# A first group with both keys in one tile, head weights in fp32 column groups, and first loads without waits

## The reference, cut to what matters

```
xn = rmsnorm(h, norm_g)
aq, ak, av, agate, iq, ik, iw, cq, ckv, kr, bgate, mg = split_proj(xn @ w_in)
ik = rope(ik, IDX_ROT)      # 64 columns, key of the indexer
iw = iw * IDX_HEADS ** -0.5 # 16 columns, one weight per head of the indexer
kr = rope(kr, ROPE_DIM)     # 64 columns, rotary key of the second branch
score = sum over heads of relu(iq . ik * IDX_DIM ** -0.5) * iw
```

## Time and profile before

| | |
|---|---|
| median of 3 runs | 825.13 us (824.22 to 826.7) |
| profiled execution | 825.64 us, of which the span shown by the profile is 823.8 |
| mean granted TensorE clock | 0.998 of full speed |
| TensorE busy | 810.5 us, 98% of the span |
| VectorE, ScalarE, GpSimd busy | 524.4, 360.1, 47.2 us |
| moved by DMA | 139.84 MB, 170 GB/s over the span |

### The profile page before, as it was taken

The page is one execution under the profiler, slowest core; times in us unless marked ns, Lnnn a source line. Parts: engine busy times, 40 slices in busy tenths (PEclk is TensorE's granted clock), DMA queues, the critical chain, the costliest instruction groups (busy, mean ns, idle before and its releaser), DMA issues.

```text
span 823.8 us, 14766 instructions
## 1 busy us (share of the span) xinstructions
PE 810.5 (98%) x5953; PEld 769.8 (93%) x5953; DVE 524.4 (64%) x845; ACT 360.1 (44%) x527; POOL 47.2 (6%) x53
## 2 busy tenths in 40 slices
PE   7999999999999999999999999999999999999996
PEld 7999999999999998999999999999999999876774
DVE  5798866899876565456544444556566666645665
ACT  6734444453455583244433434343443333334433
POOL 1222102013100000000000000000000000100001
PEclk9999999999999999999999999999999999999999
DMA  9956345544633466134574555455545545464323
GB/s 319 348 179 204 118 154 175 173 132 153 205 106 113 150 255 196 53 103 138 174 251 153 165 182 163 154 159 165 185 138 169 160 151 199 157 265 160 147 103 115
DMA packets 114356, 139.84 MB, mean 170 GB/s; under 512 B 2785, under 2 KB 99041, under 8 KB 113633
## 3 DMA queue, kind: packets, MB, share of 16 engines
q1 hardware_dynamic: 112384, 131.61, 48.8%
q0 software_dynamic: 1776, 7.53, 2.5%
q10 hardware_dynamic: 144, 0.01, 0.0%
HBM read 135.44 MB, written 3.69 MB: 169 GB/s over the span
## 4 chain that ended last, share of the span: by engine, by line
PE 96%; DMA 1%; DVE 1%; ACT 1%; issue 0%; SPq 0%; ACTq 0%; DVEq 0%
PE ps L551 25%; PE ps L550 25%; PE ps L552 25%; PE ps L896 4%; PE ps L898 3%; PE ps L897 3%; PE ps L908 2%; PE ps L747 1%; PE ps L653 1%; PE ps L719 1%; PE ps L702 1%; DMA raw<-in_w_small 1%; PE ps L708 1%; PE ps L738 1%; PE ps L706 1%; DMA x_t<-in_x_t 0%
## 5 line engine op out<-in xcount | busy, mean ns | idle before, releaser
L947 ACT CAST w_hi<-raw 128x1024 fp32r<-128x1024 f32 (+1 forms) x232 | 239.9, 1041 | 324.6 <-PE ps L552 255.5
L1272 DVE TENSOR_TENSOR w_lo<-raw,w_hi 128x1024 fp32r<-128x1024 f32 (+1 forms) x232 | 280.7, 1229 | 155.0 <-ACT w_hi L947 153.3
L550 PE MATMUL ps<-x_hi,w_hi 128*128 128x288 f32 x1248 | 371.3, 298 | 4.2 <-DVE x_lo L1299 4.2
L551 PE MATMUL ps<-x_lo,w_hi 128*128 128x288 f32 x1248 | 368.1, 295 | 0.0
L552 PE MATMUL ps<-x_hi,w_lo 128*128 128x288 f32 x1248 | 367.8, 295 | 0.0
L550 PEld LDWEIGHTS ps<-x_hi,w_hi 128*128 128x128 f32 x1248 | 234.7, 188 | 6.7 <-DVE w_lo L1295 4.5
L551 PEld LDWEIGHTS ps<-x_lo,w_hi 128*128 128x128 f32 x1248 | 234.7, 188 | 0.2
L552 PEld LDWEIGHTS ps<-x_hi,w_lo 128*128 128x128 f32 x1248 | 234.5, 188 | 0.0
L552 PE MATMUL ps<-og_hi,w_lo 128*128 128x288 f32 x256 | 75.9, 296 | 0.0
L550 PE MATMUL ps<-og_hi,w_hi 128*128 128x288 f32 x256 | 75.7, 296 | 0.0
L551 PE MATMUL ps<-og_lo,w_hi 128*128 128x288 f32 x256 | 74.6, 292 | 0.0
(11 more groups left out here) (256 smaller groups left out, 758.0 us busy)
## 6 DMA issues: line engine op xcount, KB each, us to landing
raw<-in_w_in SPq DMA_DIRECT2D x76, 1024.0 KB, 5.0
raw<-in_w_out SPq DMA_DIRECT2D x16, 1024.0 KB, 5.0
raw<-in_w_o_a SPq DMA_DIRECT2D x8, 1024.0 KB, 5.0
raw<-in_w_o_b SPq DMA_DIRECT2D x8, 1024.0 KB, 5.2
raw<-in_w_uv SPq DMA_DIRECT2D x4, 1024.0 KB, 5.6
raw<-in_w_uq SPq DMA_DIRECT2D x4, 768.0 KB, 4.7
raw<-in_w_ukt SPq DMA_DIRECT2D x2, 1024.0 KB, 6.2
raw<-in_w_uk SPq DMA_DIRECT2D x2, 1024.0 KB, 5.0
```

Source lines behind the costliest of these rows:

```text
L550: nc.tensor.matmul(out, hi, x_h, start=first, stop=False)
L551: nc.tensor.matmul(out, hi, x_l, start=False, stop=False)
L947: nc.scalar.copy(w_hi[:, step % 2, cols], raw[:, step % RAW, cols]).then_inc(hi_done, pieces_done(q))
L1272: nc.vector.tensor_tensor(w_lo[:, step % 2, cols], raw[:, step % RAW, cols], w_hi[:, step % 2, cols].bitcast(F32), ALU.subtract)\
```

## The change

The unused columns go: `w_small` becomes 128 columns, ik in the first 64 and kr in the last 64, so the first group has one tile (three matmuls per k), in PSUM bank 4. The head weights get a 16-column input of their own, `w_iw`, loaded by ScalarE's queue. GpSimd clears a tile with 32 columns per k (`w_iwg`) and writes `w_iw` times `norm_g` into 16 of them. TensorE multiplies it with the uncast `x_t` in plain fp32, k modulo 4 choosing a group of 32 output partitions of bank 5, in three visits: k = 0 to 3 before the first group's k = 4, k = 4 to 7 before k = 8, and k = 8 to 15 before k = 12. VectorE scales all 128 rows of bank 5 into `iw_q`, and three matmuls with `sel`, which has four identity matrices of 16 columns below each other, add the four partial sums and turn them, in place of the transposes. SyncE issues all twelve first loads without a wait, and the first load of G_IQ in two halves of four k, each with a semaphore.

```
+def small_cols(k, n):
+    first = 1024 * (k % KH // QUARTER) + P * (k % QUARTER)
+    return slice(first, first + P * n)
...
-        small = ps[:, 4:6, 0:NTOK]
+        small = ps[:, 4, 0:NTOK]
...
             for i, (k0, n) in enumerate(PARTS):
-                if i >= 3:
-                    sp.wait_ge(x_landed[i - 3], 16)
-                dst = raw[:, k0 // KH, 256 * (k0 % KH):256 * (k0 % KH + n)].rearrange("p (k n) -> p k n", k=n)
+                dst = raw[:, k0 // KH, small_cols(k0, n)].rearrange("p (k n) -> p k n", k=n)
...
                 if j < 2:
                     sp.wait_ge(x_landed[len(PARTS) - 3 + j], 16)
+                if j == 0:
+                    for p, done in enumerate((first_landed, raw_landed[2])):
+                        dst = raw[:, 2, 1024 * p:1024 * p + 1024].rearrange("p (k n) -> p k n", k=PIECE)
+                        sp.dma_start(dst, w_in[:, PIECE * p:PIECE * p + PIECE, col:col + 256]).then_inc(done, 16)
+                    continue
...
             pool.memset(ones[:], 1.0).then_inc(ones_set, 1)
+            pool.memset(w_iwg[:], 0.0).then_inc(iw_cleared, 1)
+            pool.wait_ge(iw_cleared, 1)
+            pool.wait_ge(consts_landed, 16)
+            pool.wait_ge(iw_landed, 16)
+            pool.tensor_tensor(w_iwg[:, :, 0:IDX_HEADS], w_iw[:],
+                               norm_g[:].rearrange("p (k o) -> p k o", o=1).broadcast_to([P, KD, IDX_HEADS]), ALU.mult)\
+                .then_inc(iw_weighted, 1)
...
+            pool.dma_start(sel[:], d["sel"]).then_inc(ident_landed, 16)
...
+            pool.wait_ge(iw_ready, 3)
...
+            def head_weights(parts):
+                pe.wait_ge(iw_weighted, 1)
+                for i in parts:
+                    pe.wait_ge(x_landed[i], 16)
+                    k0, n = PARTS[i]
+                    for k in range(k0, k0 + n):
+                        c = 32 * (k % 4)
+                        last = nc.tensor.matmul(ps[c:c + 32, 5, 0:NTOK], w_iwg[:, k, :], x_t[:, k, :], start=k < 4,
+                                                stop=k >= KD - 4)
+                last.then_inc(iw_ready, 1)
             for k in range(KD):
-                half, row_tile = k // KH, k % KH
+                if k and k % QUARTER == 0:
+                    head_weights({4: (0, 1), 8: (2, 3), 12: (4, 5)}[k])
...
-                for m in range(2):
-                    cols = slice(m * P, (m + 1) * P)
-                    last = three(small[:, m, :], hi[:, row_tile, cols], lo[:, row_tile, cols], x_hi[:, k, :],
-                                 x_lo[:, k, :], k == 0, k == KD - 1)
+                hi, lo = (w[:, half, small_cols(k, 1)] for w in (w_hi, w_lo))
+                last = three(small, hi, lo, x_hi[:, k, :], x_lo[:, k, :], k == 0, k == KD - 1)
...
-                last = nc.tensor.transpose(ps[0:n, 6, tt * P:(tt + 1) * P], ik_z[:, t0:t0 + n], ident[:])
+                last = nc.tensor.matmul(ps[0:n, 6, tt * IDX_HEADS:(tt + 1) * IDX_HEADS], iw_q[:, t0:t0 + n], sel[:],
+                                        start=True, stop=True)
...
+                if isinstance(it, int) and q == 4:
+                    act.wait_ge(first_landed, 16)
+                else:
+                    act.wait_ge(raw_landed[step % RAW], landed(step, it))
...
+                if group == G_SMALL:
+                    nc.scalar.copy(z_stage[:, 0, 0, :], small)
+                    nc.scalar.copy(z_stage[0:ROPE, 0, 1, :], small[ROPE:2 * ROPE, :]).then_inc(pair_read, 1)
+                    return
...
             act.dma_start(norm_g[:], d["norm_g"]).then_inc(consts_landed, 16)
+            act.dma_start(w_iw[:], d["w_iw"]).then_inc(iw_landed, 16)
...
-            settled(nc.vector.tensor_tensor(ik_z[64:P, :], z[64:P, :], x_rstd[64:P, 0, :], ALU.mult))
+            dve.wait_ge(iw_ready, 3)
+            settled(nc.vector.tensor_tensor(iw_q[:], ps[:, 5, 0:NTOK], x_rstd[:, 0, :], ALU.mult))
```

More of the change, by code:

```diff
@@ L265, in hybrid_layer @@
         x_t, _ = at("x_t", [P, KD, NTOK], at_y)
-        x_sq, x_ss, x_var, x_root, d_end = row(at_x, ("x_sq", [P, KD, NTOK]), ("x_ss", [P, NTOK]), ("x_var", [P, NTOK]),
-                                               ("x_root", [P, NTOK]))
+        x_sq, x_ss, x_var, x_root, w_iw, w_iwg, d_end = row(at_x, ("x_sq", [P, KD, NTOK]), ("x_ss", [P, NTOK]), ("x_var", [P, NTOK]),
+                                               ("x_root", [P, NTOK]), ("w_iw", [P, KD, IDX_HEADS]),
+                                               ("w_iwg", [P, KD, 32]))
         assert d_end <= at_y
@@ L273, in hybrid_layer @@
             ("work", [P, 3, PAST + DEC]))
-        cq_hi, cq_lo, ckv_tok, iw_tok, top8, iw_four, _ = row(
+        cq_hi, cq_lo, ckv_tok, iw_tok, top8, iw_four, sel, _ = row(
             at_l, ("cq_hi", [P, KL, NTOK], F32R), ("cq_lo", [P, KL, NTOK], F32R), ("ckv_tok", [P, 3, LORA]),
-            ("iw_tok", [P, 3, IDX_HEADS]), ("top8", [P, 2, 8]), ("iw_four", [P, 4]))
+            ("iw_tok", [P, 3, IDX_HEADS]), ("top8", [P, 2, 8]), ("iw_four", [P, 4]),
+            ("sel", [P, IDX_HEADS]))
         ckv_past, score, s_end = row(at_y, ("ckv_past", [P, KL, PAST]), ("score", [P, 3, PAST + DEC]))
@@ L280, in hybrid_layer @@
         lora_z, _ = at("lora_z", [P, 2, KL, NTOK], at_f)
-        ik_t, ik_z, kr_swap, _ = row(at_x, ("ik_t", [P, NKEY]), ("ik_z", [P, NTOK]), ("kr_swap", [P, NTOK]))
+        ik_t, ik_z, kr_swap, iw_q, _ = row(at_x, ("ik_t", [P, NKEY]), ("ik_z", [P, NTOK]), ("kr_swap", [P, NTOK]),
+                                           ("iw_q", [P, NTOK]))
         ckv_hi, ckv_lo, _ = row(at_x, ("ckv_hi", [P, KL, NKEY], F32R), ("ckv_lo", [P, KL, NKEY], F32R))
@@ L366, in hybrid_layer @@
         quarters_moved = sem("quarters_moved")
+        iw_landed, iw_cleared, iw_weighted, iw_ready, first_landed = (
+            sem(n) for n in ("iw_landed", "iw_cleared", "iw_weighted", "iw_ready", "first_landed"))
         ident_landed, idx_out = sem("ident_landed"), sem("idx_out")
@@ L614, in _ @@
                 pe.wait_ge(xlo_done, k + 1)
-                hi, lo = weights(half, KH)
-                for m in range(2):
-                    cols = slice(m * P, (m + 1) * P)
-                    last = three(small[:, m, :], hi[:, row_tile, cols], lo[:, row_tile, cols], x_hi[:, k, :],
-                                 x_lo[:, k, :], k == 0, k == KD - 1)
+                hi, lo = (w[:, half, small_cols(k, 1)] for w in (w_hi, w_lo))
+                last = three(small, hi, lo, x_hi[:, k, :], x_lo[:, k, :], k == 0, k == KD - 1)
                 if k % QUARTER == QUARTER - 1:
@@ L944, in piece_hi @@
                 step, cols = q // 2, piece_cols(q)
-                act.wait_ge(raw_landed[step % RAW], landed(step, it))
+                if isinstance(it, int) and q == 4:
+                    act.wait_ge(first_landed, 16)
+                else:
+                    act.wait_ge(raw_landed[step % RAW], landed(step, it))
                 act.wait_ge(step_done, freed_by(q) + 2 * RAW * it)
@@ L961, in to_stage @@
                     act.wait_ge(stage_used, group - 3)
-                src = small if group == G_SMALL else pair(group)
-                nc.scalar.copy(z_slot(group), src).then_inc(pair_read, 1)
+                nc.scalar.copy(z_slot(group), pair(group)).then_inc(pair_read, 1)
             act.dma_start(norm_g[:], d["norm_g"]).then_inc(consts_landed, 16)
+            act.dma_start(w_iw[:], d["w_iw"]).then_inc(iw_landed, 16)
             act.wait_ge(ones_set, 1)
@@ L1289, in _ @@
             for i, (k0, n) in enumerate(PARTS):
-                half, cols = k0 // KH, slice(256 * (k0 % KH), 256 * (k0 % KH + n))
+                half, cols = k0 // KH, small_cols(k0, n)
                 if i in (0, 2):
@@ L1830 @@
     w = arrays["in_w_in"]
-    first = np.concatenate([w[:, COL_IK:COL_IK + P], w[:, COL_KR:COL_KR + P]], axis=1)
-    arrays["in_w_small"] = np.ascontiguousarray(first.reshape(KD, P, 2 * P).transpose(1, 0, 2))
+    first = np.concatenate([w[:, COL_IK:COL_IK + IDX_DIM], w[:, COL_KR:COL_KR + ROPE]], axis=1)
+    arrays["in_w_small"] = np.ascontiguousarray(first.reshape(KD, P, P).transpose(1, 0, 2))
+    head_weights = w[:, COL_IW:COL_IW + IDX_HEADS]
+    arrays["in_w_iw"] = np.ascontiguousarray(head_weights.reshape(KD, P, IDX_HEADS).transpose(1, 0, 2))
+    arrays["in_sel"] = np.ascontiguousarray(np.tile(np.eye(32, IDX_HEADS, dtype=np.float32), (4, 1)))
     past_k = arrays["in_cache_a_k"].reshape(PAST, A_KV, A_DIM)
```

7 lines of the change are left out of this document (4 added, 3 removed).

## The result

The changed kernel takes 822.74 us (median of 16 runs, 822.34 to 824.62), the kernel before, run beside it, 826.07 (16 runs, 823.81 to 827.24). The ratio is 0.9969, 95% interval 0.9962 to 0.9977: about 2.6 us of 825 are gone (1.9 to 3.1). The ratio is not the quotient of the two medians, which would be 0.9960: the 16 runs of the kernel before fall into two bunches, seven of 823.8 to 825.2 and nine of 826.0 to 827.2. By the medians 3.3 us are gone, against the 825.13 from which the prediction subtracts it is 2.4, and the profiled executions, 825.64 (span 823.8) and 822.36 (span 820.6), are 3.3 apart. Forecast were 4.45. So the direction was right and the size was not, by whichever of these measures.

A forecast was written before the change was run, and what follows sets the result against it. TensorE was taken to bound the kernel (96% of the chain), with data landings setting G_IQ's start after the change. Savings 4.8 - 0.2 - 0.15 = 4.45 us from the median 825.13 gave 820.7 us, range 819.3 to 823.0.

The forecast's parts named there:

- 4.8 - 0.2 - 0.15 = 4.45: Whole saving in us: earlier G_IQ start, less a stall at its second step, less extra records of the sel matmuls.
- Saving 22.27 - 17.5 = 4.8: First stage: G_IQ's first matmul moves from 22.27 to 17.5 us, saving 4.8, from 4.0 to 5.6.
- rival (b): Head weights: the column groups run in turn, TensorE needs 14.8 us, kernel at 823.5; chance 0.04.
- Rival (c): First loads: without waits they disturb one another, x_t's last part lands at 15 to 17, kernel 822.3 to 824.3; chance 0.08.
- Rival (d): First stage into G_IQ: TensorE's clock falls to 1.2 GHz; beyond 13.9 us of it, over 0.3% slower; chance 0.06.
- 825.13 - 4.45: Whole kernel: the saving of 4.45 us subtracted from the median of the kernel before gives 820.7 us.
- The landing of the fifth token part, 11.2: First loads: token part five (k = 8 to 11) lands at 11.2 us, between 10.5 and 11.9.
- Until 8.0 us 8.0 x 258 GB/s = 2.06 MB: First loads: bytes moved by 8.0 us in the earlier profile, from which the new landing times were worked out.
- SyncE's waits: beyond the rate above this saves nothing: First loads: dropping SyncE's three waits gains nothing beyond the assumed 0.375 MB/us, as the queue was nearly full before.
- What could be late next: G_IQ's second step: second half of the first w_in load lands near 17.0, TensorE stalls 0.2 us, at most 1.2.
- rival (a): G_IQ's second step: second half-load or the squares chain is late, 1 to 2 us given back, 821.7 to 822.7; chance 0.13.
- `sel`, I take 0.15 (0 to 0.5): Turning the head weights: three fp32 matmuls need two records each instead of one, 0.15 us more.

The follow-up runs named there:

- e9: The kernel before the change, unchanged, run once more for a second profile; 824.96 us (one run, span 823.2).
- e3: Changed kernel with head weights of k = 0 to 3 only, twelve of the sixteen fp32 matmuls left out; 822.57 us, ratio 0.9959.
- e1: Changed kernel with the old loads: SyncE's waits before the last six first loads back, first w_in load in one transfer; 824.98 us, ratio 0.9998.
- e2: Kernel before with the new loads alone: no waits before the first loads, first w_in load in two halves; 824.17 us, ratio 0.9982.
- e4: Changed kernel with three transposes and a VectorE sum over the four column groups in place of the matmuls with sel; 822.62 us, ratio 0.9961.
- e5: Changed kernel with token part five (k = 8 to 11) loaded in two transfers, a semaphore each; 822.83 us, ratio 0.9973.
- e8: Changed kernel with the w_iw transfer issued after ScalarE's first table load instead of ahead of it; 822.79 us, ratio 0.9976.
- e18: Changed kernel, unchanged, once more on another chip; 822.90 us (6 runs), ratio 0.9968.
- e15: Changed kernel with later rope table, 16 warm-up matmuls, token part five split, transposes plus VectorE sum for sel, without three VectorE rotary products; time not in the text.

## Why the prediction was wrong: the path held, the sizes on it did not

**The step that failed** is the sum "4.8 - 0.2 - 0.15 = 4.45", above all its first term, "Saving 22.27 - 17.5 = 4.8". G_IQ began at 18.10 and not at 17.5, which leaves 4.17 us in the pair of profiles, and only 3.45 against e9, in which G_IQ of the kernel before began near 21.55. `sel`, put at 0.15, measured 0.48, and a wait in VectorE's block near 60 us, which the sum lacked, took 0.18. The wait and the path that were forecast are the ones found; these errors all went the same way.

**What held.** TensorE's work of the first group fell to 48 matmuls and 32 records in three visits; the column groups run four at once (0.62 for four matmuls, 1.11 for eight; with the 0.10 ahead of each visit, which the forecast of 0.8, 0.8 and 1.3 had counted in, 0.72 and 1.21); in turn four alone would have been 1.9 us, so rival (b) is out. That the start of G_IQ is set by data and not by TensorE holds: e3 takes two visits away and moves it by 0.03. ScalarE's and VectorE's chain from the token part's landing to G_IQ was forecast at 6.3 us (17.5 less 11.2) and measured 6.31. The x_t part's last transfer landed at 13.85 (5.94 + 7.9; forecast 13.4, 12.7 to 14.1). Rival (c), that the unwaited loads disturb one another, did not come in its strong form: without the new loads the gain is gone (e1). In a weak form it may have: fewer bytes had moved by 8 us in e2 too (term 2). Rival (d), the clock, did occur, in three profiles of variants (e4, e5, e8), for 3 to 4 us only; as TensorE had time to spare there, it cost 0.2 us of G_IQ's start at most, and the case beyond 13.9 us never came.

**The terms one by one**, in the order of the sum:

1. "825.13 - 4.45", with 4.45 read from a profile of 825.64. The 22.27 of that profile holds 0.7 us of late landings that e9 does not have. Against the ratio this is the largest single error; against the difference of the medians, 3.3 us, it is none, so how much of it is an error rests on one more profile of a kernel whose runs spread over 3 us. The prediction saw the 0.5 between profile and median and passed over it; a saving that ends in a landing time can't be taken from one execution and subtracted from the median of others.
2. The landing of the fifth token part, 11.2, was 11.79: G_IQ at 18.10, 0.6 us. It was within its own bounds (10.5 to 11.9), but the middle was wrong, and it was so before 8 us already: the fourth part, put at 8.2, landed near 8.9, where SyncE's next issue, which waits for it, stands. The table by stretch of after:

```profile
0.00:8.00 8.00, 5.13 (x27) 4.76 (x28) 2.57 (x6) 4.43 (x10) 1.50 (x7) 1.00 0.73 223
8.00:14.00 6.00, 4.92 (x41) 3.58 (x41) 4.90 (x12) 4.81 (x11) 0.00 (x0) 1.00 1.04 395
14.00:30.00 16.00, 15.68 (x125) 14.60 (x124) 14.46 (x19) 13.54 (x16) 4.72 (x8) 1.00 1.08 382
```

   "Until 8.0 us 8.0 x 258 GB/s = 2.06 MB" became 8.0 x 223 = 1.78 MB. From 4 to 8 us the DMA engines are full in both (share 1.02 and 1.04) and move 335 GB/s against 375. The transfers of `w_small` of the first parts are half as large (128 KB over 128 partitions, 1 KB each, for 2 KB), and 1 KB pieces of `w_iw` came in beside them. But the piece size is not the whole of it: e2, with the old 2 KB pieces and without `w_iw`, moved 335 GB/s from 4 to 8 us as well, and 239 until 8.0; e1, with the new pieces and the old waits, 322 and 218. So the issues without waits and the new pieces each go with a lower rate there; neither was varied any finer. The rate behind 8 us (401 to 11.79, for 375) gave some of it back.
3. "SyncE's waits: beyond the rate above this saves nothing". e1 shows up to 2.2 us of G_IQ's start behind them, together with the halved load. The error didn't touch the sum, since the sum assumed a full queue, but whoever kept the waits on the strength of that sentence would have lost the gain.
4. "What could be late next": the second half of the first w_in load was cast at 16.8, piece 6 was ready at 23.7 (22.48 and half of 2.36), and TensorE asked for it at 24.45, G_IQ having begun 0.6 later than forecast. So no stall came there, and rival (a) did not either. What came late was the load behind it, whose landing the text did not work out (issued at 11.8, landed after 8.7 us), and it was felt 40 us further on, in VectorE's block: 0.18 us in the profile of after, with the restart, and up to 1.4 in others. The text had looked for the next late thing only up to 28 us. With the 0.10 of G_IQ's restart it makes 0.28 for 0.2.
5. "`sel`, I take 0.15 (0 to 0.5)": 0.48, the upper end. With 16 moving columns in each, it isn't the columns that take it; what share the change of form has was not tried by itself.
6. The end of the span: 0.2 us behind TensorE's last matmul, cause open.

By profiles: 4.77 forecast for G_IQ's start, less 0.6 (2), 0.28 (4 with the restart), 0.48 (5), 0.2 (6) is 3.2. Less the 0.7 of (1), with 0.1 for rounding, it is the 2.6 of the ratio. The chances put 0.66 on 819.6 to 821.4, where the time is not, and 0.84 on a time under 822.65, which the median of 822.74 misses by 0.09. It lies in the stated range of 819.3 to 823.0 only because that reached up for rivals (a) and (c), and neither came as it was described: that is luck.

## What to carry to other kernels

A saving at the start of a chain is worth what the tightest engine behind it lets through: look, as far as the prologue's order reaches, for the engine without idle time (here VectorE from 39 to 66 us) and ask how late its block may start. Take a landing time from more than one execution, and subtract from the time of the execution it was read in; the two profiles of the same kernel before differ by 0.72 us at the very number from which the saving was counted. When work is moved off the bounding engine, where it is put in the other engine's order counts as much as its length: the same reduction cost 0.32 us behind a rotation and nothing that shows ahead of it.

## What the runs showed of the hardware

- fp32 matmuls of 288 columns in four column groups: four take 0.62 us and eight 1.11. So a round of four costs 0.49, what one full-width matmul costs, and a visit 0.13 on top. Counted as in the prediction, with the gap ahead of it (8.56 to 8.79 is 0.23 for 0.13), that is 0.23, near the 0.26 read from the earlier trace rows; the matmul behind it is followed after 0.24 in place of 0.13 (9.41 to 9.65), another 0.1 that neither count has.
- A matmul that follows a wait is followed by the next after 0.21 to 0.24 us instead of 0.13: 0.21 behind the waits for `x_lo` at 6.64 and 13.05, 0.24 behind that for `w_lo` at 18.10.
- TensorE's clock in the first group, in 20 profiles. With 10 warm-up matmuls the grant fell to 0.50 near 8 us in e4, e5 and e8, after idle stretches of 1.57, 1.53 and 1.76 us and a first real matmul at 7.10, 6.83 and 7.25. In e1 and e18 (0.98 and 1.22 us, first matmul at 6.63 and 6.87) the column stands at 1.00, but the matmuls stand 0.24 us apart until 9.4 and 9.6. The other eight, seven with 0.4 to 1.1 us and the profile of after with 1.70 (first matmul at 6.64), have neither. So the length of the idle stretch alone does not part them. None of the seven profiles with 16 has a slow stretch there. The Trainium skill (TensorE: Matmul & The Clock Gate, HAM oscillation) names such waits between bursts as the cause; the three profiles with a fall agree, that of after does not.
- Two pieces of `w_lo` take VectorE 2.36 us at 16.82 and 3.60 at 58.74, where GpSimd's product on `z_cos` (58.88, 2.38 us) runs beside them: 1.2 us for one piece of two. In e15, where that product began only at 58.11, the pair at 56.60 took 2.36; but one piece at 54.64 of after took 1.23 beside such a product (54.77). GpSimd's product of this size took 1.43 us at 51.63 and 2.40 at 54.77. So the two engines hold each other up at some starts and not at others; no run varies this alone.
- An issue on ScalarE's DMA queue left at 1.26 us though it stood behind an activation in program order (e8).
